# Low halves in scalar_tensor_tensor, output projection and second norm in one block by token tiles, float32r tiles at multiples of 512 bytes

## The reference

```python
def rms_norm(x, gain):
    return x * lax.rsqrt(jnp.mean(x * x, axis=-1, keepdims=True) + NORM_EPS) * gain
...
mod = (silu(c) @ w_ada + b_ada)
shift1, scale1, gate1, shift2, scale2, gate2 = jnp.split(mod, 6, axis=-1)
h = rms_norm(x, g_norm_mix) * (1.0 + scale1) + shift1
x = x + gate1 * hybrid_mixer(h, ...)
h = rms_norm(x, g_norm_ffn) * (1.0 + scale2) + shift2
x = x + gate2 * peer_ffn(h, w_peer_q, peer_keys, peer_u, peer_v)
...
def peer_block(hb, w_q, keys, u, v):
    q = (hb @ w_q).reshape(T, 8, 2, 128)
    s = jnp.einsum('thpd,pkd->thpk', q, keys)
    ...
    act = gelu(jnp.einsum('thkd,td->thk', u[idx], hb))
    return jnp.einsum('thk,thkd->td', g * act, v[idx])
```

## Time and profile before

| | |
|---|---|
| time, median of 3 executions | 3359.67 us (3352.54 to 3361.2) |
| the profiled execution | 3354.98 us |
| its span | 3353.2 us |
| its mean granted TensorE clock | 0.961 of full speed |
| PE busy | 3139.0 us, 94% |
| DVE busy | 2361.4 us, 70% |
| POOL busy | 1647.8 us, 49% |
| ACT busy | 1022.6 us, 30% |

### The profile page before, as it was taken

The page is one execution under the profiler, slowest core; times in us unless marked ns, Lnnn a source line. Parts: engine busy times, 40 slices in busy tenths (PEclk is TensorE's granted clock), DMA queues, the critical chain, the costliest instruction groups (busy, mean ns, idle before and its releaser), DMA issues. The chain is left out here.

```text
span 3353.2 us, 44573 instructions
## 1 busy us (share of the span) xinstructions
PE 3139.0 (94%) x14956; PEld 2545.7 (76%) x14956; DVE 2361.4 (70%) x4281; ACT 1022.6 (30%) x1184; POOL 1647.8 (49%) x1337
## 2 busy tenths in 40 slices
PE   6999589895999999999999699999999999999997
PEld 3789465584888888788888577877777877787776
DVE  4512565433578888766666488888888888888888
ACT  2110234423233333444444222222222222222221
POOL 2000224403333324333333577777777777777774
PEclk7999778997999999999999899999999999999999
DMA  5620000023232223454554799999999999999997
GB/s 211 203 69 26 10 13 26 7 101 115 88 106 101 88 88 110 144 177 164 191 185 161 252 298 306 303 299 302 301 305 300 313 301 300 304 303 300 294 308 283
DMA packets 328228, 650.03 MB, mean 194 GB/s; under 512 B 169648, under 2 KB 170944, under 8 KB 325184
## 3 DMA queue, kind: packets, MB, share of 16 engines
q1 hardware_dynamic: 235584, 342.28, 32.2%
q0 software_dynamic: 91392, 272.96, 23.2%
q10 hardware_dynamic: 1152, 33.55, 2.4%
HBM read 573.18 MB, written 75.50 MB: 193 GB/s over the span
## 5 line engine op out<-in xcount | busy, mean ns | idle before, releaser
L2074 DVE SCALAR_TENSOR_TENSOR total<-ex_ring,ex_pick,total 128x1024 f32<-128x1024 f32 x512 | 650.9, 1292 | 202.7 <-DMA ex_ring<-peer_v_dram,sp_row 194.6
L1933 POOL DMA_INDIRECT ex_pick<-act_scratch,sp_place x512 | 563.8, 1101 | 175.8 <-issue 155.8
L1938 POOL DMA_INDIRECT ex_ring<-peer_v_dram,sp_row x512 | 565.8, 1105 | 156.1 <-issue 133.8
L1966 PE MATMUL ex_dots<-h_hi_b,ex_uhi 128*128 128x512 f32 x1024 | 401.3, 392 | 25.0 <-ACT ex_uhi L2008 13.7
L1966 PE MATMUL ex_dots<-h_lo_b,ex_uhi 128*128 128x512 f32 x1024 | 400.7, 391 | 0.0
L1815 DVE TENSOR_SCALAR gm_b_hot<-gm_iota,second_T,gate_T 128x128 f32<-128x128 f32 x512 | 257.7, 572 | 172.3 <-PE gm_prod L1759 168.6
L1339 POOL TENSOR_TENSOR ga_ulo<-ga_u,ga_uhi 128x1024 fp32r<-128x1024 f32 x72 | 173.0, 2406 | 341.8 <-ACT ga_uhi L1333 341.7
L2025 ACT ACTIVATE ex_whi<-ex_dots 128x512 fp32r<-128x512 f32 x128 | 76.8, 600 | 845.8 <-DVE ex_dots L2053 845.8
L1969 PE MATMUL ex_dots<-h_hi_b,ex_ulo 128*128 128x512 f32 x1024 | 252.9, 389 | 0.0
L1339 POOL TENSOR_TENSOR ra_ulo<-ra_u,ra_uhi 128x1024 fp32r<-128x1024 f32 x56 | 140.9, 2518 | 215.9 <-ACT ra_uhi L1333 215.9
L1966 PEld LDWEIGHTS ex_dots<-h_hi_b,ex_uhi 128*128 128x128 f32 x1024 | 193.7, 189 | 66.4 <-ACT ex_uhi L2008 14.2
(11 more groups left out here) (290 smaller groups left out, 6693.0 us busy)
## 6 DMA issues: line engine op xcount, KB each, us to landing
ex_u<-peer_u_dram SPq DMA_DIRECT2D x128, 512.0 KB, 5.6
ex_v<-peer_v_dram SPq DMA_DIRECT2D x128, 512.0 KB, 8.4
ga_u<-peer_u_dram SPq DMA_DIRECT2D x72, 512.0 KB, 3.6
gate_scratch<-gm_out ACTq DMA_DIRECT2D x8, 4096.0 KB, 12.5
ex_g<-gate_scratch SPq DMA_DIRECT2D x128, 256.0 KB, 6.9
ra_u<-peer_u_dram SPq DMA_DIRECT2D x56, 512.0 KB, 3.5
act_scratch<-ga_act SPq DMA_DIRECT2D x72, 256.0 KB, 2.2
w_in_raw<-w_ada_dram SPq DMA_DIRECT2D x64, 256.0 KB, 3.6
```

The lines of the kernel that those rows point to most:

```text
L1933: nc.gpsimd.indirect_dma_start(weights[:, i:i + 1], None, places, bass.IndirectOffsetOnAxis(ap=picks[:, i:i + 1], axis=0)).then_inc(pick_i ...
L1938: nc.gpsimd.indirect_dma_start(ring[:, i], None, rows, bass.IndirectOffsetOnAxis(ap=which[:, RING * s + i:RING * s + i + 1], axis=0)).then ...
L1966: nc.tensor.matmul(dots[:, c], uhi[:, c, kk], b[:, kk], start=kk == 0 and b is hi, stop=False)
L2074: nc.vector.scalar_tensor_tensor(total[:, t], ring[:, i], weights[:, bass.ds(PER * s + i, 1)], total[:, t], ALU.mult, ALU.add).then_inc(ro ...
```

## The change

There are three edits.

**1. experts.** Four operations of DVE per chunk, the three low halves and the product with the gates, are written as scalar_tensor_tensor in place of tensor_tensor. A low half becomes (high x -1) + full. Both tensors are still read from SBUF (for the weights' low half and the gates, one from PSUM), shapes and order are the same.

```diff
+                def low_part(dst, high, full):
+                    return nc.vector.scalar_tensor_tensor(dst, high.bitcast(F32), -1.0, full, ALU.mult, ALU.add)
...
-                    nc.vector.tensor_tensor(ulo[:, c], u[:, c], uhi[:, c].bitcast(F32), ALU.subtract).then_inc(ulo_ready, 1)
+                    low_part(ulo[:, c], uhi[:, c], u[:, c]).then_inc(ulo_ready, 1)
...
-                    nc.vector.tensor_tensor(dots[:, c], dots[:, c], g[:, c], ALU.mult).then_inc(weighted, 1)
+                    nc.vector.scalar_tensor_tensor(dots[:, c], g[:, c], 1.0, dots[:, c], ALU.mult, ALU.mult).then_inc(weighted, 1)
```

```diff
-        units = [(s, t) for s in range(2) for t in range(NT)]
+        units = [(s, 2 * p + b) for p in range(NT // 2) for s in range(2) for b in range(2)]
...
                 for t in range(NT):
+                    if t >= SLOTS:
+                        sp.wait_ge(lo2_ready, t - SLOTS + 1)
+                    sp.dma_start(slot(t), rows(d["x"], t)).then_inc(x_in[t % SLOTS], 16)
...
                 for p in range(0, NT, 2):
+                    for b in range(2):
+                        residual(2 * p + b)
+                        if p:
+                            modulate(p - 2 + b)
+                    for b in range(2):
+                        residual(2 * p + 2 + b)
+                        if p + b + 2 < NT:
+                            split_low(p + b + 2)
+                        normalise(p + b)
+                modulate(NT - 2)
+                modulate(NT - 1)
...
                     mm.then_inc(y_ready, 1)
+                    if s == 0:
+                        if t + 2 < NT:
+                            turn(t + 2)
+                        if t >= 2:
+                            turn_normed(t - 2)
+                turn_normed(NT - 2)
+                turn_normed(NT - 1)
```

More of the change, by code:

```diff
@@ L19 @@
 AX = mybir.AxisListType
+LINE = 512
 P = 128
@@ L200, in on_gpsimd @@
             self.split_low(pool, n)
[L203 to L229, removed]
 def adaln_and_norm(nc, k, d, constants, hi, lo):
@@ L567, in _ @@
             def _(sp):
-                w_out.load(sp, 0)
+                w_out.load(sp, 0, w_out.first[0])
             @block.tensor
@@ L1152, in _, with split_in_place @@
                                               scores_in[m % 2]).then_inc(att_ready, 1)
-class OutWeights:
[L1158 to L1166, removed]
+def split_in_place(nc, ctx, name, shape, side="left"):
+    start = -(-nc.sbuf_base // LINE) * LINE
+    raw = ctx.enter_context(nc.sbuf_tensor(name, shape, F32, side=side, align_bytes=LINE))
+    low = nc.alloc_sbuf_tensor_at(name + "_low", shape, F32R, offset=nc.sbuf_top if side == "right" else start)
+    return raw, low
@@ L1190, in project_out, with rows, columns, slot @@
+        units = [(s, 2 * p + b) for p in range(NT // 2) for s in range(2) for b in range(2)]
+        ends = [units.index((1, t)) for t in range(NT)]
+        def rows(a, t):
+            return a[t * P:(t + 1) * P, :]
+        def columns(parts, t):
+            return parts[t // NA][:, :, t % NA * P:(t % NA + 1) * P]
+        def slot(t):
+            return x[:, t % SLOTS]
+        def blocks(t):
+            return x[:, t % SLOTS].rearrange("p (k c) -> p k c", k=KD)
         with nc.Block() as block:
@@ L1192, in _ @@
             def _(sp):
[L1193 to L1199, removed]
+                w_out.load(sp, 1, raw[1])
+                for t in range(NT):
+                    if t >= SLOTS:
+                        sp.wait_ge(lo2_ready, t - SLOTS + 1)
+                    sp.dma_start(slot(t), rows(d["x"], t)).then_inc(x_in[t % SLOTS], 16)
@@ L1201, in _, with store @@
+                load_ahead(sp)
             @block.gpsimd
             def _(pool):
[L1203 to L1207, removed]
+                def store(t):
+                    pool.wait_ge(x1_ready, ends[t] + 1)
+                    pool.dma_start(rows(x1, t), o[:, t]).then_inc(stored, 16)
@@ L1209, in _, with split_low @@
+                def split_low(t):
+                    pool.wait_ge(hi2_ready, t + 1)
+                    nc.gpsimd.tensor_tensor(columns(los, t), blocks(t), columns(his, t).bitcast(F32),
+                                            ALU.subtract).then_inc(lo2_ready, 1)
+                for p in range(0, NT, 2):
+                    store(p)
+                    store(p + 1)
+                    split_low(p)
+                    split_low(p + 1)
+                pool.wait_ge(stored, 16 * NT)
             @block.scalar
@@ L1210, in _, with split_w @@
             def _(act):
[L1211 to L1224, removed]
+                def split_w(s, q):
+                    if q == 0:
+                        act.wait_ge(w_out.arrived[s], 16)
+                    at = slice(q * KQ, (q + 1) * KQ)
+                    nc.scalar.activation(whi[:, s, at], raw[s][:, at], ACT.Copy).then_inc(whi_ready, 1)
```

213 lines of the change are left out of this document (139 added, 74 removed).

## The result

The changed kernel takes 3338.65 us (median of 8, 3332.02 to 3345.17) where the kernel before takes 3358.01 us: a ratio of 0.9938, 95% interval 0.9927 to 0.9949. It is faster by 0.6%, not by the 6% of the forecast. Ratios here leave out one execution of the changed kernel that took 3510.95 us at a granted clock of 0.84.

The account below looks back on a forecast made before the run. POOL was taken to bound experts, PE's matmul pitch route and gate matrix. Terms 107 + 35 + 18 + 15 + 28 + 4 = 207 us off 3354.98 gave 3148, as median 3153 us; range 3118 to 3262.

Parts of the forecast that it names:

- Step 1: Experts: scalar_tensor_tensor leaves POOL alone and alignment speeds PE, so the chunk goes from 11.29 to 10.45 us; -107 us.
- a long one: Experts: a POOL indirect DMA of 1.36 us, not 0.94, claimed to occur always beside a tensor_tensor of DVE.
- Rival B: Experts: any DVE operation with two SBUF inputs holds POOL, beat stays 11.29 us; rest -100, 3260 us; chance 0.06.
- The forecast of 1275 us for POOL without holds: Experts: 1024 indirect DMAs at 1.245 us each, 9.96 us per chunk, putting POOL below PE.
- Rival C: Experts: DMA becomes the bound; at 315 GB/s the chunk is 11.02 us, experts -34, total -134, 3226 us; chance 0.12.
- the 332 of the forecast: Experts: DMA rate in GB/s needed at 10.45 us per chunk, called possible but near.
- rival A: Alignment only removes the difference between operands: experts -42, route -13, input projection -3, merged stage -28; 3274 us; chance 0.13.
- Step 2: Route, gate matrix, input projection: alignment brings 512-column float32r matmuls to 216 ns; -35, -18 and -15 us.
- the other bound, 226.5: Pitch in ns of 512-column float32r matmuls if only the difference between operands counts; route -13, gate matrix 0.
- Step 3: Projection and second norm merged: route begins at 785.7 for 813.6 us, -28; alignment there another -4.
- the 4 for its alignment: Merged projection and norm: 384 matmuls each 10.7 ns shorter when aligned, -4 us.

Follow-up runs that it names:

- the tensor_scalar: Changed kernel with a tensor_scalar (one SBUF input) in place of the low halves of u and v; that operation takes 0.69 us for 1024 elements.

## Why the prediction was wrong

**Step 1, experts (-107 forecast, +24 measured).** The step that failed is: "a long one always has a tensor_tensor of DVE beside it, one with L2074 alone never". I grouped POOL's operations by what starts in them, and not by what they start in. Of the 191 that row additions held, 126 have a low half of v next in the program and 63 the product with the gates, so a long one is nearly always seen with a tensor_tensor behind the row addition. The count does not bear the sentence either: two long ones have L2074 alone beside them, and 437 of the 703 short ones have a tensor_tensor. The 0.94 us beside L2074 in the earlier trace rows is a start within 0.1 us of it, and such starts are many (294 before): POOL's cycle is 1.245 us and two row additions take 2.5, so that the two can fall in step. Rival B was the right one, with 0.06. The Trainium skill (SBUF — State Buffer, "SBUF: two separate sides") has the rule: a DVE operation with two SBUF inputs takes the shared pair for the whole instruction against a GpSimd instruction that reads SBUF, and one in a two-port mode takes it too. The indirect DMAs here have their indices in SBUF tiles (`sp_row`, `sp_place`). The runs agree with both: 0.82 us behind the end in over 310 cases per kernel in either form, and the tensor_scalar, if its 0.69 us against 1.21 mean such a mode. I had weighed the rule and set it aside for a row that I misread.

What sets experts is POOL's sum. Over the thirteen profiles on chips without pauses (all have the element fetches) experts take 1316 to 1321 us plus the excess: 1481.2 - 163.3 = 1317.9 and 1505.1 - 187.7 = 1317.4, 1451.8 - 132.4 = 1319.4 and 1560.5 - 244.1 = 1316.4 at the ends. The rest is 1024 x 0.945 = 968, 1023 gaps of 0.305 = 312, and 37 to 42 behind POOL's last: POOL waits for nothing in any of them. The forecast of 1275 us for POOL without holds was right in kind, but no edit took a hold away. Rival C did not come to bear: without the element fetches the DMAs kept up at PE's beat, at 312 GB/s. No run reached the 332 of the forecast.

The changed kernel has 14 to 24 us more excess. The pitch of rival A and the holds of rival B both came true, which the prediction had only apart: 13 for route, 3 and 28 are 44 us. The spans differ by 12; of the 32 us that are missing, 24 are this excess, a term that stood at nothing, and 7 gated linear attention. The cause of the excess stays open. The form of the operations is out (165.9 alone). Alignment and the new places each came with more (174.3, 180.9), and the row additions have 18 us more of it (125 for 107); how a place of a tile shifts the phase was not shown.

**Step 2, the pitch.** "I take 216, since the float32 matmuls show that PE itself adds only 2.7 and nothing else in the rows explains 13" is the step that failed; the other bound, 226.5, was right (rival A, 0.13). Route: 2112 x 6 = 13 us forecast at that bound, 12.4 to 13 measured; gate matrix 0 against 1.1; input projection -0.8, since the 1344 matmuls of 256 columns lost 2.5 ns each (+3.4) and the 432 of 512 columns won 5.5 (-2.4); where the other -1.8 are I did not trace. The float32 matmuls' 2.7 ns don't carry over to float32r: the 13.3 are the same at 512 and 256 columns, and with 64 weight columns they are 16.7. So in these rows it is a cost per float32r matmul, and its cause none of the runs shows. The 215.7 ns that the Trainium skill (TensorE: Matmul & The Clock Gate, "Wait — 56ns, not 53.3ns?") gives for 512 columns is reached by no float32r row here; the float32 rows agree with it, at two clocks a column.

**Step 3, the merged block.** Right: 28 forecast and 29 measured, and the 4 for its alignment is 0 (227 ns before and after). This is not luck of opposite errors: the first product came 4.4 us behind the block's start, as forecast (668.7 - 664.3), the products took 98.1 us for 99.2, and from the last product to the last low half it was 15.3 us for 14.8. DVE waited 4 us for x three times (3.97, 4.21, 4.34), and PE never for that.

**Not in the forecast.** Gated linear attention took 7 us more. The granted clock between 400 and 420 us, of the changed kernel and of the same with tensor_tensor:

```profile
400.00:420.00 20.00, 20.00 (x100) 13.29 (x102) 9.60 (x25) 1.49 (x3) 13.73 (x16) 0.59 0.00 0
```

```profile
400.00:420.00 20.00, 20.00 (x164) 14.45 (x164) 15.13 (x39) 2.39 (x4) 14.31 (x16) 1.00 0.01 2
```

PE gets through 100 matmuls where it does 164 at full clock. The mean of 0.59 is a mix of the two levels: in the changed kernel the granted clock is 1.2 GHz from 351.7 to 392.7 us, 2.4 GHz for 6.8 us, 1.2 GHz again for 17.1 us and then 2.4 GHz. In the other it rises at 394.9 and stays up for 41 us. In both PE had been idle for 25.4 us until 389.8 and 391.2. Of twelve profiles with the merged block's layout, eight have 92.2 to 95.1 us in this stage and four 84.1 to 86.2; the five of the old layout have 83.9 to 85.3. What makes the difference was not tried.

## What to carry to other kernels

When an operation on one engine has two lengths, group it by the operation in whose course it starts and measure from that one's end; a sharp constant there (0.82 us, medians within 3 ns) points at the cause, where "what is seen beside it" can merely follow program order. Count the short ones too. Between engines that hold each other, shorter single operations limit the hold (two pieces of 512: 51 us, 1.5%), but here only when all that hold were cut: the low halves alone made experts 55 us slower, and the row additions alone gained nothing (1498.7 us, beside 1505.1 and 1495.8 of the changed kernel). At 512 columns, float32r operands at the same remainder by 512 bytes gained up to 6 ns a matmul, and none went below columns / 2.4 GHz + 13 ns; at 256 columns the alignment cost 2.5.

## What I had not expected

A row addition holds POOL's indirect DMA only if that one starts about 0.1 us or more into it, and then the DMA ends 0.82 us behind it. In the kernel before it is always free of the next DVE operation, in the changed kernel in all cases but one. With pieces it often is not, and a law of the single hold that fits two kernels to 3 ns still gave 70 us where 132 came. And the chip matters: the changed kernel with pieces took 3581 us on one and 3290 on another, and in the profiles all of that lies in experts (1742.8 for 1451.8 us).
